# A two-block diffusion-transformer kernel: gate rows computed inside the gated projection, and another order of the first loads

## The reference, cut to what matters

```python
m = jax.nn.silu(c) @ w_ada + b_ada            # 6 x 1024 columns; shift, scale, gate
u_lat = modulate(x, sh1, sc1) @ w_in          # modulate: layer_norm(x) * (1 + scale) + shift
dt = softplus(u[..., OFF_DT:OFF_FNET] + dt_bias)   # 16 narrow columns of w_in
```

```python
qa, ka, va, oa, ga, qb, kb, vb = jnp.split(h @ w_in, bounds, axis=-1)
g = (ga + gate_b)                              # (direction, kind, head) per token
gates = (g[0], log_sigmoid(g[1]), g[2], log_sigmoid(g[3]))
# per chunk of 128 tokens, per direction:
bcum = cumsum(fc);  d_log = bcum[t] - bcum[s] + ic[s]
m_t = maximum(bcum + m, max_s d_log);  s = (q k^T) * exp(d_log - m_t)
m_new = maximum(b_last + m, max(b_last - bcum + ic))   # carried from chunk to chunk
```

## Time and profile before

| | us |
|---|---|
| runs of the kernel before (3) | 2682.61 to 2685.97, median 2683.45 |
| the profiled execution, whole | 2679.2 |
| its span, first to last instruction | 2677.4 |
| PE busy in the span | 2401.1 (90%) |

### The profile page before, as it was taken

The page is one execution under the profiler, slowest core; times in us unless marked ns, Lnnn a source line. Parts: engine busy times, 40 slices in busy tenths (PEclk is TensorE's granted clock), DMA queues, the critical chain, the costliest instruction groups (busy, mean ns, idle before and its releaser), DMA issues. The chain is left out here.

```text
span 2677.4 us, 34959 instructions
## 1 busy us (share of the span) xinstructions
PE 2401.1 (90%) x14311; PEld 1941.2 (73%) x14311; DVE 1204.6 (45%) x1947; ACT 804.2 (30%) x1322; POOL 995.0 (37%) x609
## 2 busy tenths in 40 slices
PE   6987789999996996858798999999989798899998
PEld 4866456777775995735577888888867587688887
DVE  4518628756645006766516233232417653423322
ACT  4233334333325223324413111111124264322221
POOL 2326135555544221310025334343425001555553
PEclk8999889999997998878899999999999899899999
DMA  8460213544440121000012223343311001222221
GB/s 260 157 220 1 73 64 122 169 134 146 153 158 18 48 64 48 1 9 1 17 48 79 95 95 123 99 142 108 97 56 63 32 1 35 75 95 94 95 94 47
DMA packets 224700, 229.94 MB, mean 86 GB/s; under 512 B 7375, under 2 KB 221219, under 8 KB 224547
## 3 DMA queue, kind: packets, MB, share of 16 engines
q1 hardware_dynamic: 224211, 227.66, 26.4%
q10 hardware_dynamic: 336, 0.11, 0.0%
HBM read 225.65 MB, written 2.10 MB: 85 GB/s over the span
## 5 line engine op out<-in xcount | busy, mean ns | idle before, releaser
L1095 POOL TENSOR_TENSOR w_lo<-ring,w_hi 128x1024 fp32r<-128x1024 f32 x128 | 306.9, 2398 | 426.0 <-ACT w_hi L1090 426.0
L1090 ACT ACTIVATE w_hi<-ring 128x1024 fp32r<-128x1024 f32 x128 | 135.6, 1061 | 740.8 <-PE ps L1153 701.6
L1885 DVE SCALAR_TENSOR_TENSOR xT<-ps,mods,xT 128x512 f32<-128x512 f32 (+1 forms) x160 | 108.3, 684 | 537.1 <-PE ps L1153 475.9
L1151 PE MATMUL ps<-hidden_hi,w_hi 128*128 128x512 f32 (+1 forms) x768 | 274.0, 357 | 5.2 <-POOL hidden_lo L2235 4.9
L1152 PE MATMUL ps<-hidden_lo,w_hi 128*128 128x512 f32 (+1 forms) x768 | 272.1, 354 | 0.0
L1153 PE MATMUL ps<-hidden_hi,w_lo 128*128 128x512 f32 (+1 forms) x768 | 271.7, 354 | 0.0
L1151 PE MATMUL ps<-h_hi,w_hi 128*128 128x512 f32 (+1 forms) x720 | 256.3, 356 | 6.9 <-POOL w_lo L1095 3.0
L2157 DVE SCALAR_TENSOR_TENSOR ffn_sums<-ps,cols,ffn_sums 128x441 f32<-128x441 f32 (+2 forms) x352 | 215.0, 689 | 105.3 <-ACT ffn_sums L2080 105.3
L1152 PE MATMUL ps<-h_lo,w_hi 128*128 128x512 f32 (+1 forms) x720 | 255.0, 354 | 0.0
L1153 PE MATMUL ps<-h_hi,w_lo 128*128 128x512 f32 (+1 forms) x720 | 254.6, 354 | 0.0
L2225 DVE TENSOR_TENSOR squares<-squares 128x512 f32<-128x512 f32 (+1 forms) x72 | 143.1, 1987 | 222.6 <-ACT squares L2211 222.6
(11 more groups left out here) (447 smaller groups left out, 5206.5 us busy)
## 6 DMA issues: line engine op xcount, KB each, us to landing
ring<-in_mlp_w SPq DMA_DIRECT2D x64, 1024.0 KB, 5.3
ring<-in_ada_w SPq DMA_DIRECT2D x48, 1024.0 KB, 5.3
ring<-in_w_ada SPq DMA_DIRECT2D x24, 1024.0 KB, 9.6
ring<-in_ffn_w_up SPq DMA_DIRECT2D x22, 1024.0 KB, 7.1
ring<-in_ab_w_in SPq DMA_DIRECT2D x11, 1024.0 KB, 5.2
ring<-in_ffn_w_down SPq DMA_DIRECT2D x12, 768.0 KB, 5.7
ring<-in_w_in SPq DMA_DIRECT2D x8, 1024.0 KB, 7.6
ring<-in_c_w_in SPq DMA_DIRECT2D x6, 1024.0 KB, 5.1
```

The source lines that it names most:

```text
L1090: act.activation(w_hi[m][:, 0:x["kt"], :], ring[:, x["n"] % NS, 0:x["kt"], m * P:(m + 1) * P], ACT.Copy).then_inc(SW["w_hi"].sem, 1)
L1095: pool.tensor_tensor(w_lo[m][:, 0:x["kt"], :], ring[:, x["n"] % NS, 0:x["kt"], m * P:(m + 1) * P], w_hi[m][:, 0:x["kt"], :].bitcast(F32), ...
L1151: pe.matmul(o, w_hi[m][:, k, :], h, start=(k == 0), stop=False)
L1885: return nc.vector.scalar_tensor_tensor(x, bank, column_of(gates, t * 2 + 2 * gate + r), x, ALU.mult, ALU.add)
```

## The change

Three things are changed.

1. **Gates inside the projection.** A `Gates` object goes through `units_stage` for `ab_w_in`. DVE computes the log-sigmoid right after the bias (ACT's Exp and Ln stand at units (1, 1) and (1, 2)); PE turns the gate columns after the first unit of n = 2 (16 transposes) and of n = 3 (8), DVE copies them out and runs the scans, PE turns the results after the first unit of n = 5 (36 transposes instead of 24: the input-gate terms are turned too), and ACT takes the exponentials at (6, 0). The rows lie in buffers that the later slabs fill (oa, qb, kb). The blocks L2728 and L2816 are gone, and the transposes' block keeps 8 groups of 16; POOL clears the mLSTM states there. In the mLSTM, `front` spreads a column of input-gate terms (weights: that column broadcast to 128x128, moving: the identity) where it spread a row.
2. **The order of the first slabs.** The first `w_in` slab is the seventh of the stream instead of the fifth; six `w_ada` slabs stand ahead of it and two behind it. ACT splits it at u = 12 and u = 14.
3. **The order on SP.** The small parameters are issued in three lots with a slab between them; the narrow columns and the 14 constant matrices come behind the last `w_ada` slab of the modulation. The narrow columns are split after the norm, on ACT and on POOL; PE waits for the constant matrices at the end of the block.

```diff
-        W["ada"], W["in_0"] = add_slabs("w_ada", 0, whole, cols_of(0, 4), 1), 4
+        W["ada"], W["in_0"] = add_slabs("w_ada", 0, whole, cols_of(0, 6), 1), 6
         add_slabs("w_in", 0, whole, [OFF_XBC], 0)
-        add_slabs("w_ada", 0, whole, cols_of(4 * SLAB, 4), [1, 1, 1, 1 + 4])
+        add_slabs("w_ada", 0, whole, cols_of(6 * SLAB, 2), [1, 1 + 4])
...
             def sync(self, sp):
-                load_params(sp, 15, len(col_rows))
+                load_params(sp, 15, 20)
+                load_slabs(sp, NS + 1)
+                load_params(sp, 20, len(col_rows))
+                load_gains(sp)
+                load_slabs(sp, NS + 2)
                 load_rows(sp)
+                load_slabs(sp, NS + 5)
+                load(sp, wnarrow[:, :, :], w["w_in"][0, :, OFF_DT:OFF_DT + 16].rearrange("(k p) n -> p k n", p=P), loaded.sem)
                 load(sp, mats[:, FIRST_MATS:N_MATS, :], w["const_mats"][FIRST_MATS:N_MATS].rearrange("n p q -> p n q"), mats_in)
...
-                elif u in (8, 10):
-                    self.high(u // 2 - 4)
-                elif u == 12:
-                    self.narrow_part()
+                elif u in (12, 14):
+                    self.high(u // 2 - 6)
...
+            def pe(self, pe, n):
+                if n in (2, 3):
+                    c0, nc_ = ((0, NLAT), (NLAT, NCTX))[n - 2]
+                    self.wait(pe, *(("gate_logs", 1) if n == 2 else ("gate_kinds", 4)))
+                    for kind in range(4):
+                        for j in range(nc_):
+                            at0 = (c0 + j) * 16 + kind * 4
+                            ins = pe.transpose(ps[0:4, 4 + kind, j * P:(j + 1) * P], dt[:, at0:at0 + 4], ident)
+                        self.sig(ins, "gate_turned")
+                elif n == 5:
+                    self.wait(pe, "gate_rows", 1)
+                    for d in range(2):
+                        for c in range(NCH):
+                            o, cut = (d * NCH + c) * 4, slice(c * CH, (c + 1) * CH)
+                            for i, row in enumerate((row_m, row_b, row_i)):
+                                pe.transpose(ps[:, 4, i * N4 + o:i * N4 + o + 4], row[:, d, cut], ident[0:4, 0:4])
+                    self.sig(pe.matmul(ps[:, 4, 3 * N4:4 * N4], ones[0:4, :], ends.rearrange("p d c h -> p (d c h)"),
+                                       start=True, stop=True), "gate_cols")
...
+            def act(self, act, n, m):
+                if (n, m) == (1, 1):
+                    act.wait_ge(v_order.sem, self.abs_at)
+                    act.activation(t_a, t_a, ACT.Exp, scale=-1.0).then_inc(S["exp_ln"].sem, 1)
+                elif (n, m) == (1, 2):
+                    act.wait_ge(v_order.sem, self.one_at)
+                    act.activation(t_c, t_b, ACT.Ln).then_inc(S["exp_ln"].sem, 1)
+                elif (n, m) == (6, 0):
+                    self.wait(act, "gate_sum", 1)
+                    act.activation(em, ps[:, 4, N4:2 * N4], ACT.Exp, scale=-1.0)
+                    act.activation(carry, ps[:, 4, 3 * N4:4 * N4], ACT.Exp)
+                    self.sig(act.activation(w_all, w_all, ACT.Exp), "gate_exp")
+
+            def dve(self, dve):
+                self.logs(dve)
+                for t0, w_ in BOTH:
+                    for kind in range(4):
+                        self.wait(dve, "gate_turned", kind + 1 + (4 if t0 else 0))
+                        d, k = divmod(kind, 2)
+                        self.sig(dve.tensor_copy((row_i, row_f)[k][:, d, t0:t0 + w_], ps[0:4, 4 + kind, 0:w_]), "gate_kinds")
+                self.wait(dve, "gate_kinds", 8)
+                self.rows(dve)
+                self.wait(dve, "gate_cols", 1)
+                self.sig(dve.tensor_copy(rp, ps[:, 4, 0:N4]), "gate_rp")
...
                     for h in range(4):
-                        ins = pe.matmul(ps[:, 2 * (s % 2), h * P:(h + 1) * P], mats[0:4, SEL + h, :],
-                                        raw[:, 2 * d, t0:t0 + CH], start=True, stop=True)
+                        ins = pe.matmul(ps[:, 2 * (s % 2), h * P:(h + 1) * P],
+                                        heads_of(i_cols, d, c)[:, h:h + 1].to_broadcast([P, P]), ident,
+                                        start=True, stop=True)
```

More of the change, by code:

```diff
@@ L808, in _ @@
                         lead.sync(sp)
-                    if narrow is not None:
+                    if narrow is not None and lead is None:
                         sp.dma_start(wnarrow[:, :, :], narrow.rearrange("(k p) n -> p k n", p=P))\
@@ L873, in _ @@
                             narrow_turn()
+                        if fresh_slab and gates is not None:
+                            gates.pe(pe, n)
                         if ada and last_unit(u):
@@ L878, in _ @@
                         ada_tiles(pe, 1)
+                    if lead is not None:
+                        pe.wait_ge(mats_in, 16)
                 @block.vector
@@ L903, in _, with narrow_low @@
                         low(pool, h)
-                    if narrow is not None:
+                    def narrow_low():
                         pool.wait_ge(S["narrow_hi"].sem, S["narrow_hi"].at(1))
@@ L908, in _ @@
                             .then_inc(S["narrow_lo"].sem, 1)
+                    if narrow is not None and lead is None:
+                        narrow_low()
                     if lead is None:
@@ L2728, in program @@
-        with nc.Block() as block:
-            @block.vector
-            def _(dve):
+        by_c = lambda a: a.rearrange("p d (c n) -> p d c n", n=CH)
+        gate_rows = lambda o: big[0:4, at_oa + 2 * o * TOK:at_oa + 2 * (o + 1) * TOK].rearrange("p (d n) -> p d n", d=2)
+        row_i, row_f, row_b, row_m, keep = (gate_rows(o) for o in range(5))
+        assert at_oa + 10 * TOK <= at_k
+        n_m, N4 = 2 * NCH, 8 * NCH
+        rp, w_all, carry, em = (small[:, i * N4:(i + 1) * N4] for i in range(4))
```

194 lines of the change are left out of this document (88 added, 106 removed).

## The result

The changed kernel takes **2648.97 us** in the median of four runs (2645.27 to 2651.38); the kernel before, timed beside it, 2683.03. The ratio is 0.987 with a 95% interval of 0.985 to 0.989. In a second series it was 0.987 again (0.985 to 0.990). The forecast was 2646 in a range of 2638 to 2656.

The account below looks back on a forecast made before the run. PE, busy 90% of the span, was taken as the bound, with time to win only where it stands still or runs slow. 33.6 + 3.2 - 6.3 - 1.4 + 8.0 = 37.1 off 2679.2, plus 4.25, gave 2646 us; range 2638 to 2656.

Parts of the forecast that it names:

- three blocks: Between projection and mLSTM: logarithms' block gone 6.9, transposes' block shrinks 4.1, scans' block gone 22.6; gain 33.6 us.
- clock up in the mLSTM: mLSTM start: pauses under a microsecond leave PE at full clock; gain 3.2 us (0 to 4.3).
- spread of a column: mLSTM `front`: 128x128 weights instead of 4x128 for the spread; no cost.
- PE work in the projection: Gated projection: 60 small transposes, the product of `ends` and three breaks; cost 6.3 us (4.6 to 8.6).
- table load at the root: Query heads' first root, n = 9: ACT's table load directly ahead lengthens PE's 1.23 us wait; cost 1.3 us.
- opening: Start to first projection: last modulation slab lands at 41.5, first product at 47.6; gain 8.0 us (5 to 9.5).
- breaks and the product: Gated projection: product of `ends` and three breaks in PE's stream of products; cost 0.7 us (0 to 2).
- `gate_logs` and `gate_rows`: Gated projection: PE's waits for these counters cost nothing, with 4 and 14 us to spare.
- My own sign of being wrong: Opening: DMA rows showing the last modulation slab after 45 us would make the forecast wrong.
- issue at 22, 2.0 of start-up, five slabs of 3.2: Opening: from the fifth slab's issue, last modulation slab lands at 40.0, up to 2.5 us later if transfers run dry.
- rival of an opening that doesn't pay: Opening: slabs still land late or PE waits for parameters; gain 0 to 4 us, time 2650 to 2654; chance 0.12.
- the low clock's 3.2: mLSTM start: rival that it still starts at the low clock; price 3.2 us, time 2649; chance 0.15.

Follow-up runs that it names:

- pause20: Changed kernel plus 28 unneeded DVE copies ahead of the transposes' block; first to third mLSTM spread took 9.12 us, against 8.30 in the changed kernel.
- params_pool: Changed kernel with the 22 small loads of the second block issued on POOL's queue instead of SP's; ratio 0.987 (0.985 to 0.989).
- after_again: Changed kernel run once more, unmodified, for another trace of the opening; ratio 0.987 (0.985 to 0.990).
- opening_only: Kernel before with only the new order of the first loads (parts 2 and 3); ratio 0.998 (0.997 to 0.9995), median 2678.17 us.

## Why the prediction was right, and where it was off

The time was forecast at 2646 and came at 2649, within the range. By the steps of the sum, with what each measured:

| term | forecast | measured |
|---|---|---|
| three blocks | -33.6 | -33.6 (6.9 and 26.7) |
| clock up in the mLSTM | -3.2 (0 to 4.3) | -3.2 in this pair, 0.8 for a pause of 12.2 us |
| spread of a column | 0 | -2.3 |
| PE work in the projection | +6.3 (4.6 to 8.6) | +5.4 |
| table load at the root | +1.3 | +3.0 |
| opening | -8.0 (5 to 9.5) | -3.6 in this pair, -6.1 in the mean of nine traces |

**The blocks** came out to a tenth, because their terms were differences of starts in one trace and nothing new takes their place. **The insertions:** the 24 at 0.115 were 0.109; the 36 at 0.08 (2.9 us) were 0.062 (2.2), near the lower bound, which took half of the length at the low clock. The breaks and the product, put at 0.7, were 0.6. `gate_logs` and `gate_rows` cost nothing, as forecast.

**The root.** The step said that ACT's load stands directly ahead of the roots and makes PE's wait 1.23 + 1.3. It did, with 2.65 us, but the step left out the clock: behind the longer wait PE ran 3.4 us at the low level. The forecast priced the clock in the mLSTM and nowhere else, though every added wait could have been asked that question.

**The spread** was put at no cost, from 1.15 and 1.16 us for the two halves of `front`. Both lengths contained the cost of the switch, since each stood next to a switch. That they were the same was read as "weights of 4 rows cost the same", where they should have been held against eight products with no switch beside them (1.06 in after).

**The clock.** Its size was right in this pair, the argument only in part, since the same two steps hold up to four switches and `pause20` paid only 0.8. That pauses under a microsecond don't lower it held. Against the rule of the Trainium skill on transposes (TensorE: Matmul & The Clock Gate, "Part 4: PE-mode transpose") I set that the old block of transposes rose from the low level; the 30 large ones bear me out, the run with 72 small ones and `params_pool` with 36 speak for the rule. It deserved its chance.

**The opening** was mis-sized: the last modulation slab was to land at 41.5, within 40.0 to 42.5. In after it was issued at 32.44 and landed 12.1 us later by the view of DMAs, at 44.5, and PE used it at 45.51.

```profile
ring<-in_w_ada SPq DMA_DIRECT2D x1, 1024.0 KB, 12.1
```

My own sign of being wrong was a landing after 45: five of the six new openings stay just under it (43.4 to 44.7), after_again passes it with 45.5. The chain "issue at 22, 2.0 of start-up, five slabs of 3.2" failed in two terms. The fifth slab was issued at 23.90 and not 22: the half of the old issue time was too little, since the first lot holds the long issues. And the transfers did not run at one slab in 3.2 us behind each other: the fifth, sixth and seventh were issued 3.1 and 3.8 us apart with the small loads between them, and the window of 31 to 47 us moved 297 GB/s, not 325. From 40.0, the chain without a gap, to the landing at 44.5 lie 4.5 us: 1.9 are the later issue, and the remaining 2.6 are slower or interrupted transfers, for which I had set aside 2.5 and taken 1.5. From the landing to its use the slab waited for PE another 0.2 to 1.0 us in the six traces. The three issues of after:

```profile
23.90 0.38 SPq L315 DMA_DIRECT2D ring<-in_w_ada  x1
...
27.00 0.40 SPq L315 DMA_DIRECT2D ring<-in_w_ada  x1
...
30.81 0.43 SPq L315 DMA_DIRECT2D ring<-in_w_in  x1
```

What softened the error was luck: the base of 49.99 was the best of three old openings, whose mean is 51.5. The rival of an opening that doesn't pay, with 0 to 4 us, is what the one trace pair showed; the mean of nine traces speaks against it, the 1 to 9 us of `opening_only` do not exclude it.

The sum with the measured terms is -33.6 - 3.2 - 2.3 + 5.4 + 3.0 - 6.1 = -36.8, against 33 to 34 in the medians; the difference lies within the interval. That it stands so near the forecast's 37.1 is luck in part: the spread's 2.3 and the cheaper insertions' 0.9 made up for 1.7 at the root and 1.9 at the opening. The range held a slip too: the failed opening with its 2654 and the low clock's 3.2 at once give 2657, above the 2656 that was to take both in.

## What to carry to other kernels

Work on few partitions that depends only on a narrow slice can run on idle engines inside a PE-bound stage; price what PE gets for it from the trace, and at each wait that grows, even by 1.3 us, ask what the clock does behind it. Load an activation table early with one dummy instruction where ACT is idle. Take the opening's times from several executions before sizing a gain there, and put bytes that nobody needs yet behind those that the path waits for.

## What the runs showed of the hardware

The granted clock falls for stretches of 3.4 us and more inside the stages: 3.4 us behind the root's wait of 2.65 us, 6.8 us at one place in the SSD stage in nine traces and not in five, and up to 30.7 us (in before from 1189 us on, with PE busy for two thirds of it). The 6.8 us cost 1.7 us in 16 products and 3.4 to 3.7 us in that stage. Between spreads with weights of 4 rows and products with 128 a step lost 0.38 us over two switches, about 0.2 us each, in six of the eleven steps. 72 transposes of 4x4 in 4.46 us were followed by a low stretch though PE never stood still, 36 of them in one trace of ten. A first block whose last loads POOL issued let go 5.3 us after the last issue, 0.5 us after the last of them had landed.
